# Second feed-forward: block products for three of four up matrices, accumulating weight loads, and the rectified square on ScalarE

## The chip, the core and the metric

One NeuronCore of a Trainium2 chip runs the whole kernel. Its engines are TensorE (PE in the profile, with its weight loads as PEld), VectorE (DVE), ScalarE (ACT), GpSimd (POOL) and SyncE (SP), which here only issues transfers. The metric is the device time of one execution in microseconds, the median of several runs.

## What is computed

The program is two transformer blocks on 512 tokens of width 1024, in float32. Only the second feed-forward, its last stage, is touched:

```
h = rms_norm(x, norm_mlp)                                  # 512 x 1024
x = x + square(relu(h @ w_up)) @ w_down                    # w_up 1024 x 4096, w_down 4096 x 1024
return rms_norm(x, norm_final)
```

where `rms_norm(x, g)` is `x * rsqrt(mean(x * x) + 1e-6) * g`, row by row.

## The kernel before

**Precision.** Every float32 matrix is split into a high part, rounded to the format fp32r (a copy by ScalarE, `..._hi`), and the rest (the difference, by VectorE, `..._lo` or `..._rest`). A product is then three matmuls, high by high, low by high and high by low (`three`, lines 1471 to 1475), so each weight panel costs ScalarE one 128 x 1024 copy and VectorE one 128 x 1024 subtraction before TensorE may use it. The split weights stand in a ring of four slots (`RING`): the copy for a panel waits until the panel four places earlier has been used (`panel_done`).

**Chunks.** The 4096 hidden features are taken in four chunks of 1024 (`CHUNKS2`). A chunk has two phases.

- *Up*: eight panels `Up2(c, u)`. Panel u gives 128 features by 512 tokens: eight groups of three matmuls with 512 columns (`up`, line 2970). VectorE empties the bank with `up_evac` (line 2518): the maximum with 0 times `rrow`, the row of 1/rms of each token spread over all partitions. ScalarE squares (`square`). After every second panel, `combine` forms four sums of quarters of the activations (by tokens and by features), and `combination_hi`, `single_rest` and `sum_rest` split the seven operands into `xch` and `xcl`.
- *Down*: fourteen units `Unit2(c, j)`, which are seven block products in two halves A and B, in the order P1A, Q5A, P1B, Q5B, P6A, P6B, P2A, P2B, P7A, P7B, Q3A, Q3B, R4A, R4B. Seven products of half-size blocks take the place of eight (a scheme of Strassen's kind, with sums of weight blocks by `raw_sum`, line 2548, and sums of activations). Each unit is twelve matmuls with 512 columns. Partial results are copied from bank to bank by ScalarE (`seed`, line 2061, for which P6A waits) and added into the residual `y` by VectorE (`take`, line 2557).

**The first chunk** has more in it. After the last residual sum TensorE forms the column sums of squares, GpSimd raises them to the power -1/2, and `row(5)` spreads the result over the partitions with four transposes inside panel 2. `turn_x` transposes the residual x into token rows after panels 3 to 6 (eight transposes each), which ScalarE copies to `y`.

**Order.** All queues are written out by hand: each engine runs its list in order and waits on semaphores. SyncE loads the panels of `w_up` into four `stage` buffers (512 KB each) and the quarters of `w_down` into `raw` (1 MB each). GpSimd does no transfers.

## Time and profile before

| | |
|---|---|
| median of 3 runs | 1464.92 us (1464.87 to 1464.98) |
| the profiled execution | 1464.81 us |
| its span, first to last instruction | 1463.1 us |
| mean granted TensorE clock | 0.997 |
| TensorE, VectorE, ScalarE busy | 1451.8, 1046.4, 647.5 us |
| first up panel of the second feed-forward to the last matmul | 1124.7 to 1456.2 us of the span |

A row of a group of instructions gives the line, engine and operation, the tiles, the shapes, the count, the busy time in us and the mean duration in ns, and behind the second bar the idle time of the engine just before them with what ended it. A timeline row gives start and duration in us. Matmuls are pipelined: one lasts longer than the distance to the next, and that distance is what it costs in a stream. The same holds to a smaller degree on VectorE and ScalarE.

### The profile page before, as it was taken

To read this page: it belongs to the slowest core of one execution; us is meant where nothing else is said; L and a number is where in the kernel's file an instruction comes from. 1 tells how busy PE (TensorE), PEld (TensorE's weight loads), DVE (VectorE), ACT (ScalarE), POOL (GpSimd) and SP (SyncE) were. 2 spreads that over 40 slices of the span, in tenths; PEclk is the share of its full clock that TensorE was granted. 3 is DMA by queue.
4 is the path that set the end of the run, shared out by engine and by line. 5 is a ranking of instruction groups with operands and counts; after the bars stand their busy time and mean duration, and the time that the engine had idled before them with its cause. 6 is when DMAs were issued, how large, how long until landed. Compare 5 with 4: busy or idle time off the path is not lost.

```text
span 1463.1 us, 20051 instructions
## 1 busy us (share of the span) xinstructions
PE 1451.8 (99%) x7504; PEld 1219.1 (83%) x7504; DVE 1046.4 (72%) x1601; ACT 647.5 (44%) x923; POOL 21.6 (1%) x22
## 2 busy tenths in 40 slices
PE   9999999999999999999999999999999999999998
PEld 7878788888889888988888888888888888888886
DVE  5837764676578577767968887957656686868677
ACT  5214554324434344334634655525444543535354
POOL 0000000000000000000000000000000000000000
PEclk9999999999999999999999999999999999999999
DMA  6623222323520531430233333223215333050401
GB/s 224 247 86 101 79 71 87 92 89 106 210 87 31 186 90 41 135 97 29 86 116 87 119 96 119 73 61 124 72 32 160 142 115 116 36 181 15 173 1 58
DMA packets 38850, 148.93 MB, mean 102 GB/s; under 512 B 4168, under 2 KB 4680, under 8 KB 35572
## 3 DMA queue, kind: packets, MB, share of 16 engines
q1 hardware_dynamic: 34656, 137.90, 29.2%
q10 hardware_dynamic: 4116, 9.96, 2.0%
q8 instruction: 53, 0.87, 0.2%
q14 instruction: 25, 0.20, 0.0%
HBM read 145.72 MB, written 6.06 MB: 104 GB/s over the span
## 4 chain that ended last, share of the span: by engine, by line
PE 96%; DVE 2%; issue 1%; DMA 1%; ACT 0%; SPq 0%; POOLq 0%; ACTq 0%; POOL 0%; DVEq 0%
PE ps L1473 30%; PE ps L1474 30%; PE ps L1475 30%; PE ps L1624 1%; PE ps L1637 1%; PE ps L2834 1%; PE ps L1514 0%; DMA tables<-tables_dram 0%; DVE hl L992 0%; DMA wgu<-wgu_dram 0%; PE ps L1507 0%; PE ps L2854 0%; DVE y L2561 0%; PE ps L2994 0%; PE ps L2866 0%
## 5 line engine op out<-in xcount | busy, mean ns | idle before, releaser
L1473 PE MATMUL ps<-hh,wh 128*128 128x512 f32 x1088 | 431.4, 397 | 0.0
L1474 PE MATMUL ps<-hl,wh 128*128 128x512 f32 x1088 | 424.3, 390 | 0.0
L1475 PE MATMUL ps<-hh,wl 128*128 128x512 f32 x1088 | 424.2, 390 | 0.0
L1473 PEld LDWEIGHTS ps<-hh,wh 128*128 128x128 f32 x1088 | 204.6, 188 | 45.6 <-issue 3.9
L687 ACT ACTIVATE wh<-stage 128x1024 fp32r<-128x1024 f32 x130 | 137.1, 1057 | 234.5 <-PE ps L1475 230.1
L1475 PEld LDWEIGHTS ps<-hh,wl 128*128 128x128 f32 x1088 | 204.5, 188 | 43.5
L1474 PEld LDWEIGHTS ps<-hl,wh 128*128 128x128 f32 x1088 | 204.8, 188 | 39.6
L981 DVE TENSOR_TENSOR wl<-stage,wh 128x1024 fp32r<-128x1024 f32 x129 | 157.4, 1222 | 45.5 <-ACT wh L687 45.2
L2036 ACT ACTIVATE wh<-raw 128x1024 fp32r<-128x1024 f32 x56 | 59.4, 1060 | 73.6 <-PE ps L1475 73.5
L1475 PE MATMUL ps<-xch,wl 128*128 128x256 f32 x308 | 87.2, 283 | 0.0
L1474 PE MATMUL ps<-xcl,wh 128*128 128x256 f32 x308 | 87.2, 283 | 0.0
L1473 PE MATMUL ps<-xch,wh 128*128 128x256 f32 x308 | 87.1, 283 | 0.0
L1473 PE MATMUL ps<-wh,xch 128*128 128x512 f32 x224 | 87.1, 389 | 0.0
L1474 PE MATMUL ps<-wl,xch 128*128 128x512 f32 x224 | 87.1, 389 | 0.0
L1475 PE MATMUL ps<-wh,xcl 128*128 128x512 f32 x224 | 87.1, 389 | 0.0
L858 ACT ACTIVATE wh<-stage 128x1024 fp32r<-128x1024 f32 x40 | 42.3, 1060 | 83.0 <-PE ps L1475 82.3
L2515 DVE TENSOR_TENSOR wl<-raw,wh 128x1024 fp32r<-128x1024 f32 x56 | 68.1, 1222 | 14.3 <-ACT wh L2036 13.9
L986 DVE TENSOR_TENSOR tmp<-ps,rrow 128x512 f32<-128x512 f32 x54 | 37.2, 689 | 54.6 <-PE ps L1475 50.8
L866 ACT ACTIVATE wh<-raw 128x1024 fp32r<-128x1024 f32 (+1 forms) x42 | 40.9, 984 | 53.2 <-PE ps L1475 51.2
L1282 DVE TENSOR_TENSOR wl<-stage,wh 128x1024 fp32r<-128x1024 f32 x40 | 49.0, 1225 | 19.0 <-ACT wh L858 19.0
L1474 PEld LDWEIGHTS ps<-xcl,wh 128*128 128x128 f32 x308 | 59.1, 192 | 0.1
L1473 PEld LDWEIGHTS ps<-xch,wh 128*128 128x128 f32 x308 | 59.1, 192 | 0.1
(372 smaller groups left out, 2577.2 us busy)
## 6 DMA issues: line engine op xcount, KB each, us to landing
stage<-stream_dram SPq DMA_DIRECT2D x198, 512.0 KB, 3.7
raw<-down_dram SPq DMA_DIRECT2D x24, 1024.0 KB, 6.7
bias_lines<-bias_line ACTq DMA_DIRECT2D x1, 3840.0 KB
raw<-down_dram SPq DMA_DIRECT2D x4, 768.0 KB, 5.0
bias<-bias_lines ACTq DMA_DIRECT2D x4, 512.0 KB, 5.0
out_dram<-scaled SPq DMA_DIRECT2D x4, 512.0 KB, 3.0
x<-x_dram SPq DMA_DIRECT2D x3, 512.0 KB, 7.5
bias<-bias_lines ACTq DMA_DIRECT2D x4, 256.0 KB, 2.8
```

Source lines behind the costliest of these rows:

```text
L687: A(parts_of(b, p)[0], b.stage[:, p.stage, :], ACT.Copy).then_inc(s.hi_ready, 1)
L858: A(b.wh[:, p.slot, :], b.stage[:, p.stage, :], ACT.Copy).then_inc(s.hi_ready, 1)
L866: A(b.wh[:, p.slot, 0:p.width], b.raw1[:, QUARTER[p.j], p.half, 0:p.width], ACT.Copy).then_inc(s.hi_ready, 1)
L981: V.tensor_tensor(wl, b.stage[:, p.stage, :], f32(wh), ALU.subtract).then_inc(s.lo_ready, 1)
L986: V.tensor_tensor(dst, b.ps[:, slot, :], b.rrow[:], ALU.mult).then_inc(s.evac, 1)
L1282: V.tensor_tensor(b.wl[:, p.slot, :], b.stage[:, p.stage, :], f32(b.wh[:, p.slot, :]), ALU.subtract).then_inc(s.lo_ready, 1)
L1473: MM(out, wh, xh, start=start, stop=False, skip_group_check=True)
L1474: MM(out, wh, xl, start=False, stop=False, skip_group_check=True)
L1475: return MM(out, wl, xh, start=False, stop=stop, skip_group_check=True)
L1624: ins = MM(b.ps[:, 4 + 2 * (qb % 2) + c, 0:width], q[part, tok], k[part, 0:width], start=n == 0, stop=n == 2, skip_group_check=True)
L2036: A(b.wh[:, p.slot, :], b.raw[:, QUARTER[p.j], p.half, :], ACT.Copy).then_inc(s.hi_ready, 1)
L2515: V.tensor_tensor(b.wl[:, p.slot, :], b.raw[:, QUARTER[p.j], p.half, :], f32(b.wh[:, p.slot, :]), ALU.subtract).then_inc(s.lo_ready, 1)
```

## The change

Chunk 0 keeps its form; chunks 1 to 3 get a new up phase, and the scale of the norm is moved.

- **Up phase of chunks 1 to 3.** Instead of eight panels, two groups g = 0, 1 of seven block products each, `Block2(c, g, product)`, in the order P1, Q5, P6, P2, P7, Q3, R4. The factors are blocks of `w_up` or their sums, and quarters of h by tokens and features or their sums (`xsh`, `xsl`). A product is eight groups of three matmuls with 256 columns into one bank. ScalarE copies banks (`block_seed`, `block_copy`), VectorE takes two differences (`block_take`), and the four results are rectified and squared on ScalarE (`rectify_bank`, `rectify_taken`). Then `block_sums` and the splits `block_singles_hi`, `block_sums_hi`, `block_singles_rest`, `block_sums_rest` make the operands of the down phase. Those of group 1 run at the start of the down phase.
- **Sums of h.** In chunk 0 ScalarE scales x by `norm_mlp` in place (`scale_x`, eight operations), VectorE forms four sums of quarters (`x_sums`), and `x_sums_hi` (4 copies of 128 x 1024) and `x_sums_rest` (4 subtractions) split them.
- **Weight sums.** For chunks 1 to 3, up and down, a half needs four sums: two are now made by transfers that add to their target, issued by GpSimd (`add_first`, `add_third`, 512 KB each), two by VectorE (`second_sum`, `fourth_sum`). SyncE loads five plain transfers of 512 KB for each half.
- **Scale.** The up panels are no longer multiplied by `rrow`. ScalarE rectifies straight from the bank, and `take` multiplies by 1/mean (`r2`, `nr2`) for each token, as two operations of 512 columns instead of one of 1024. `row(5)`, its power on GpSimd and the wait of the first evacuation for it are gone. `turn_x` moves to the places after panels 0 to 3. `grow` is loaded in the last chunk.

```diff
+def weight_block(b, p):
+    if p.product in (Q5, P6):
+        return b.raw_sum[:, p.half, :]
+    return b.raw[:, {P1: 0, P7: 1, Q3: 2, P2: 3, R4: 3}[p.product], p.half, :]
...
 # SyncE, chunks 1 to 3 (the loads of the next up weights in the down phase are alike)
+        for h in range(2):
+            sp.wait_ge(s.lo_ready, Block2(c, h, P1).index + 1)
+            block(c, h, True, 0)
+            sp.wait_ge(s.summed.sem, s.summed.at(summed_by(Block2(c, h, R4), R4)))
+            base(c, h, True)
+            for r, product in ((1, P7), (2, Q3), (3, R4)):
+                sp.wait_ge(s.lo_ready, Block2(c, h, product).index + 1)
+                block(c, h, True, r)
...
 # GpSimd
+    def add_first(c, h, unit):
+        lap = 2 * (c - 1) + unit
+        pool.wait_ge(s.base_in[h].sem, s.base_in[h].at(16 * lap + 16))
+        if lap:
+            pool.wait_ge(s.added_in[h], 32 * lap)
+        G.dma_start(b.raw_sum[:, h, :], weights(c, h, unit, 1), accum_op=ALU.add).then_inc(s.added_in[h], 16)
...
 # ScalarE, chunk 0
+        if u in (4, 5):
+            for k in range(4 * (u - 4), 4 * (u - 4) + 4):
+                scale_x(k)
+        if u in (6, 7):
+            x_sums_hi(2 * (u - 6))
+            x_sums_hi(2 * (u - 6) + 1)
...
 # ScalarE, chunks 1 to 3, one group
+            block_seed(at(P1))
+            block_hi(at(P7))
+            if before:
+                block_sums_hi(before, 0)
+            block_copy(at(Q5), BANK_D[g], 0)
+            block_hi(at(Q3))
+            if before:
+                block_sums_hi(before, 1)
+            block_copy(at(P6), BANK_B[g], 1)
+            block_hi(at(R4))
...
 # ScalarE, after group 1
+        last = Block2(c, 1, R4)
+        block_hi(Unit2(c, P6A))
+        block_sums_hi(last, 0)
+        block_hi(Unit2(c, P6B))
+        block_sums_hi(last, 1)
         seed(c)
...
 # VectorE, chunk 0 (loop over the eight panels), and after it
+        if u == 6:
+            x_sums()
+    for n in range(4):
+        x_sums_rest(n)
+    unit_lo(Unit2(0, P6A))
...
 # VectorE, after group 1
+        block_sums(last, 0)
+        block_singles_rest(last)
+        block_lo(Unit2(c, Q5B))
+        block_sums_rest(last, 0)
+        second_sum(Unit2(c, Q5B))
+        block_lo(Unit2(c, P6A))
+        block_sums(last, 1)
+        block_lo(Unit2(c, P6B))
...
 # TensorE, one group
+                block(c, g, P1, opens=True)
+                pe.wait_ge(s.taken.sem, s.taken.at(6 * (c - 1) + 4 + g))
+                block(c, g, Q5, opens=True)
+                pe.wait_ge(s.block_copied.sem, s.block_copied.at(3 * n + 1))
+                block(c, g, P6)
+                block(c, g, P2)
+                pe.wait_ge(s.block_copied.sem, s.block_copied.at(3 * n + 3))
+                block(c, g, P7)
+                block(c, g, Q3)
+                pe.wait_ge(s.block_taken.sem, s.block_taken.at(2 * n + 1))
+                block(c, g, R4)
```

How the queues read at three places follows, the tiles by their names and the semaphores that a row waits for in brackets.

**ScalarE, chunk 0, panels 6 and 7, before.** `wh` is the high part of a weight block, `mix<-tmp` the square, `xch<-mix` the splits, `y<-ps` the copy of turned x:

```order
L2036 ACTIVATE wh<-raw 128x1024 [waits panel_done,x_raw_in0]
L2045 ACTIVATE mix<-tmp 128x512 [waits act2_ready,evac]
L2059 ACTIVATE y<-ps 128x1024 [waits line_done_x_turned]
L2036 ACTIVATE wh<-raw 128x1024 [waits panel_done,v_normed_summed,x_raw_in0]
L2045 ACTIVATE mix<-tmp 128x512 [waits evac]
L2052 ACTIVATE xch<-mix 128x768 [waits acted2]
L2054 ACTIVATE xch<-mix 128x1024 [waits va_gelu_combined]
```

The same place now. `tmp<-ps` is the new rectification, `xsh<-x` the new copies of the sums of h:

```order
L2135 ACTIVATE wh<-raw 128x1024 [waits panel_done,x_raw_in0]
L2157 ACTIVATE tmp<-ps 128x512 [waits acted2,panel_done]
L2162 ACTIVATE mix<-tmp 128x512 [waits act2_ready,evac]
L2185 ACTIVATE xsh<-x 128x1024 [waits lo_ready,acted]
L2185 ACTIVATE xsh<-x 128x1024
L2135 ACTIVATE wh<-raw 128x1024 [waits panel_done,v_normed_summed,x_raw_in0]
L2157 ACTIVATE tmp<-ps 128x512 [waits acted2,panel_done]
L2162 ACTIVATE mix<-tmp 128x512 [waits evac]
L2168 ACTIVATE xch<-mix 128x768 [waits acted2]
L2170 ACTIVATE xch<-mix 128x1024 [waits va_gelu_combined]
L2185 ACTIVATE xsh<-x 128x1024 x2
```

Between the square of panel 6 and the weight copy of panel 7 there are now two copies that wait for `x_sums` of VectorE (semaphore `acted`).

**ScalarE, end of the up phase of chunk 1, before** (`ps<-ps` is `seed`):

```order
L2045 ACTIVATE mix<-tmp 128x512 [waits evac]
L2052 ACTIVATE xch<-mix 128x768 [waits acted2]
L2054 ACTIVATE xch<-mix 128x1024 [waits va_gelu_combined]
L2036 ACTIVATE wh<-raw 128x1024 [waits panel_done,v_normed_summed,x_raw_in0] x2
L2068 ACTIVATE ps<-ps 128x1024 [waits ln_pow_taken,panel_done]
L2036 ACTIVATE wh<-raw 128x1024 [waits panel_done,x_raw_in3] x2
```

The same place now (`block` holds the four results of a group, `spare1` and `spare2` the sums of them):

```order
L2236 ACTIVATE xch_155<-block_167 128x2x768 [waits acted2]
L2150 ACTIVATE wh_53<-raw_sum_166 128x1024 [waits panel_done,added_in1]
L2150 ACTIVATE wh_53<-raw_sum_166 128x1024 [waits panel_done,v_normed_summed]
L2243 ACTIVATE xch_155<-spare1_168 128x2x2x256 [waits va_gelu_combined]
L2150 ACTIVATE wh_53<-raw_sum_166 128x1024 [waits panel_done,v_normed_summed]
L2243 ACTIVATE xch_155<-spare2_169 128x2x2x256 [waits va_gelu_combined]
L2195 ACTIVATE ps<-ps 128x1024 [waits conved,ln_pow_taken,panel_done]
L2150 ACTIVATE wh_53<-raw_161 128x1024 [waits panel_done,x_raw_in3]
```

Two weight copies and two splits stand now ahead of `seed`; the second split waits for a sum of VectorE (`combined`).

**VectorE, the same place, now** (before, the two weight differences of P6A and P6B followed the last `sum_rest` at once):

```order
L2802 TENSOR_TENSOR spare1_168<-block_167 128x2x256 [waits acted2]
L2803 TENSOR_TENSOR spare1_168<-spare1_168,block_167 128x2x256 [waits steps]
L2793 TENSOR_TENSOR xcl_156<-block_167,xch_155 128x2x768 [waits act2_hi]
L2736 TENSOR_TENSOR wl_54<-raw_sum_166,wh_53 128x1024 [waits hi_ready]
L2817 TENSOR_TENSOR xcl_156<-spare1_168,xch_155 128x2x2x256 [waits act2_hi,va_gelu_combined]
L2743 TENSOR_TENSOR raw_sum_166<-raw_sum_166,raw_161 128x1024 [waits load2]
L2736 TENSOR_TENSOR wl_54<-raw_sum_166,wh_53 128x1024 [waits hi_ready]
L2807 TENSOR_TENSOR spare2_169<-block_167 128x2x256 [waits va_gelu_combined]
L2809 TENSOR_TENSOR spare2_169<-block_167,spare1_168 128x2x256 [waits steps]
L2736 TENSOR_TENSOR wl_54<-raw_sum_166,wh_53 128x1024 [waits hi_ready]
```

The sum for which that second split waits (`spare2`, row 9) has eight operations ahead of it since the last square.

## Rows read from the trace of the kernel before

**Rows 1.** The page: busy time of TensorE, and the chain that ended last.

```profile
PE 1451.8 (99%) x7504; PEld 1219.1 (83%) x7504; DVE 1046.4 (72%) x1601; ACT 647.5 (44%) x923; POOL 21.6 (1%) x22
...
PE 96%; DVE 2%; issue 1%; DMA 1%; ACT 0%; SPq 0%; POOLq 0%; ACTq 0%; POOL 0%; DVEq 0%
```

**Rows 2.** What TensorE waited for, the whole span (total, times, longest, in us).

```profile
PE ps L1530 <- DVE rrow L1007: 1.6, 1, 1.6
```

**Rows 3.** Timeline of the down phase: start, duration in us; matmuls with 512 columns.

```profile
1260.21 0.19 PEld L1474 LDWEIGHTS ps<-wl,xch 128*128 128x128 f32 x1
1260.43 0.39 PE L1474 MATMUL ps<-wl,xch 128*128 128x512 f32 x1
...
1262.70 0.39 PE L1475 MATMUL ps<-wh,xcl 128*128 128x512 f32 x1
```

**Rows 4.** Timeline of TensorE, first feed-forward: products with 256 columns.

```profile
450.03 0.28 PE L1473 MATMUL ps<-xch,wh 128*128 128x256 f32 x1
...
454.71 0.28 PE L1473 MATMUL ps<-xch,wh 128*128 128x256 f32 x1
```

**Rows 5.** Timeline of TensorE around `row(5)` in chunk 0.

```profile
1137.11 0.60 PE L1514 MATMUL ps<-consts,small 128*128 128x128 f32 x4
1137.46 0.48 PE L1473 MATMUL ps<-hh,wh 128*128 128x512 f32 x1
```

**Rows 6.** Timeline of VectorE, end of the up phase of chunk 0.

```profile
1173.36 0.69 DVE L2525 SCALAR_TENSOR_TENSOR tmp<-ps,rrow 128x512 f32<-128x512 f32 x1 [2.81 <-PE ps L1475]
...
1176.35 0.42 DVE L2534 TENSOR_TENSOR mix<-mix 128x256 f32<-128x256 f32 x1
1176.80 0.42 DVE L2535 TENSOR_TENSOR mix<-mix 128x256 f32<-128x256 f32 x1
...
1180.29 2.35 DVE L2515 TENSOR_TENSOR wl<-raw,wh 128x1024 fp32r<-128x1024 f32 x2
```

**Rows 7.** Timeline of ScalarE, the same stretch.

```profile
1177.26 1.06 ACT L2054 ACTIVATE xch<-mix 128x1024 fp32r<-128x1024 f32 x1 [1.36 <-DVE mix L2535]
1178.23 2.15 ACT L2036 ACTIVATE wh<-raw 128x1024 fp32r<-128x1024 f32 x2
1181.52 1.01 ACT L2068 ACTIVATE ps<-ps 128x1024 f32<-128x1024 f32 x1 [1.15 <-PE ps L1475]
```

**Rows 8.** Groups of VectorE from 1120 us on: busy us, mean ns of one.

```profile
L2515 DVE TENSOR_TENSOR wl<-raw,wh 128x1024 fp32r<-128x1024 f32 x56 | 68.1, 1222 | 14.3 <-ACT wh L2036 13.9
...
L2525 DVE SCALAR_TENSOR_TENSOR tmp<-ps,rrow 128x512 f32<-128x512 f32 x32 | 21.9, 688 | 47.7 <-PE ps L1475 41.8 <-ACT rrow L703 5.8
...
L2539 DVE TENSOR_TENSOR xcl<-mix,xch 128x768 fp32r<-128x768 f32 x16 | 15.2, 951 | 0.0
...
L998 DVE TENSOR_TENSOR sumsq<-sumsq,tmp 128x512 f32<-128x512 f32 x2 | 1.4, 685 | 0.0
```

**Rows 9.** Groups of ScalarE from 1120 us on.

```profile
L2036 ACT ACTIVATE wh<-raw 128x1024 fp32r<-128x1024 f32 x56 | 59.4, 1060 | 73.6 <-PE ps L1475 73.5
...
L2045 ACT ACTIVATE mix<-tmp 128x512 f32<-128x512 f32 x32 | 19.9, 621 | 6.7 <-DVE tmp L2525 6.7
...
L2052 ACT ACTIVATE xch<-mix 128x768 fp32r<-128x768 f32 x16 | 13.6, 848 | 0.5
```

**Rows 10.** Busy time and granted clock (PEclk) of TensorE in stretches of the opening.

```profile
5.06:8.47 3.41, 1.86 (x5) 1.00 1.03 385
8.47:11.88 3.41, 3.41 (x8) 0.50 0.73 292
```

**Rows 11.** Timeline of TensorE in the opening.

```profile
7.68 1.13 PE L1536 MATMUL ps<-onehot,tables 32*12 32x512 f32 x2 [1.55 <-DMA tables<-tables_dram]
...
10.61 0.63 PE L1475 MATMUL ps<-hh,wl 128*128 128x512 f32 x1
11.04 0.63 PE L1473 MATMUL ps<-hh,wh 128*128 128x512 f32 x1
```

**Rows 12.** Transfers from 1150 to 1300 us: count, KB each, us to landing.

```profile
stage<-stream_dram SPq DMA_DIRECT2D x13, 512.0 KB, 3.6
```

More of the change, by code:

```diff
@@ new lines, in quarter, with weights, base, block @@
+    def quarter(r):
+        sp.dma_start(b.raw[:, r, :, :], dram["down2"][0, r]).then_inc(s.raw_in[r].sem, 16)
+    def weights(c, h, unit, r):
+        return dram["down2"][c, r, :, h, :] if unit else dram["up2"][c - 1, h, r]
+    def base(c, h, unit):
+        sp.dma_start(b.raw_sum[:, h, :], weights(c, h, unit, 0)).then_inc(s.base_in[h].sem, 16)
+    def block(c, h, unit, r):
+        sp.dma_start(b.raw[:, r, h, :], weights(c, h, unit, r)).then_inc(s.block_in[h][r].sem, 16)
+    for u in range(RING, KT):
+        up_row(u)
@@ L2068, in seed, with block_seed @@
         A(b.ps[:, 2:4, :], b.ps[:, 0:2, :], ACT.Copy).then_inc(s.seeded.sem, 1)
[L2070 to L2084 removed]
+    def block_seed(p):
+        act.wait_ge(s.panel_done, p.index + 1)
+        act.wait_ge(s.taken.sem, s.taken.at(6 * (p.c - 1) + 4 + p.half))
+        A(b.ps[:, BANK_A[p.half], :], b.ps[:, BANK_B[p.half], :], ACT.Copy).then_inc(s.block_copied.sem, 1)
@@ new lines, in block_sums_hi @@
+    def block_sums_hi(p, first):
+        act.wait_ge(s.combined.sem, s.combined.at(PAIRS2 + 2 * p.number + 1 + first))
+        sums = x_quarters((b.spare1, b.spare2)[first][:])[:, :, 0, 0, :].rearrange("p (b n) c -> p n b c", n=2)
+        A(b.xch[:, 2 * p.half:2 * p.half + 2, 3 + first:7:2, :], sums, ACT.Copy).then_inc(s.act2_hi, 1)
+    for u in range(KT):
+        if u < RING:
+            up_hi(Up2(u + RING))
+        else:
+            unit_hi(Unit2(0, u - RING))
+        square(u)
+        if u % 2:
+            combination_hi(u // 2)
+        if u < TT:
+            copy_x(u)
+        if u in (4, 5):
[4 more added lines that the diff above has]
+            x_sums_hi(2 * (u - 6) + 1)
@@ new lines, in block2_vector @@
+    up_lo(Up2(RING))
+    dve.wait_ge(s.mean_ready, 5)
+    st.link(V.reciprocal(b.r2, b.mean))
+    st.link(V.tensor_scalar(b.nr2, b.r2, -1.0, None, ALU.mult))
+    for u in range(KT):
+        if u >= RING:
+            unit_lo(Unit2(0, u - RING))
+        elif u:
+            up_lo(Up2(u + RING))
+        if u % 2:
+            combine(u // 2)
+            single_rest(u // 2)
+        if u == RING:
+            raw_sum(0, 1, 0, 1)
+        elif u == RING + 1:
+            raw_sum(0, 2, 0, 2)
+        elif u == RING + 2:
+            raw_sum(0, 1, 1, 3)
+        elif u == RING + 3:
+            raw_sum(0, 2, 1, 4)
+        if u % 2:
+            sum_rest(u // 2)
+        if u == 6:
+            x_sums()
@@ new lines, in block2_vector @@
+    for n in range(4):
+        x_sums_rest(n)
+    unit_lo(Unit2(0, P6A))
+    unit_lo(Unit2(0, P6B))
+    unit_lo(Unit2(0, P2A))
+    raw_sum(1, 2, 0, 5)
+    unit_lo(Unit2(0, P2B))
+    raw_sum(1, 2, 1, 6)
+    unit_lo(Unit2(0, P7A))
+    raw_sum(3, 0, 0, 7)
+    dve.wait_ge(s.x_copied.sem, s.x_copied.at(TT))
+    take(0, 1, P6B, early, right, 0, b.nr2)
+    unit_lo(Unit2(0, P7B))
+    raw_sum(3, 0, 1, 8)
+    take(0, 2, Q5B, late, right, 4, b.r2)
+    unit_lo(Unit2(0, Q3A))
+    unit_lo(Unit2(0, Q3B))
@@ L2654, in block2_vector @@
     last_take(0)
[L2655 removed]
+    row_scale(2, 5, 3)
     row_mean(0)
```

540 lines of the change are left out of this document (368 added, 172 removed).

## The prediction

> **What bounds the kernel now.** I read the page first: TensorE is busy for 1451.8 of 1463.1 us and makes up 96% of the chain that ended last [rows 1]. Then its waits: the longest in the whole span is 1.6 us, and none falls in the second feed-forward [rows 2]. So a matmul less is time saved, and every wait that is added on TensorE is time lost. I then looked at how far apart matmuls start, since their durations overlap: with 512 columns 0.227 us (ten distances from 1260.43 to 1262.70) [rows 3], with 256 columns 0.120 us (39 distances from 450.03 to 454.71) [rows 4]. A half-width matmul costs 53% of a full one, not 50%. Last, VectorE and ScalarE, whose work must now fit a shorter phase: the durations of their forms and how they follow each other [rows 6 to 9].
>
> **Part 1, the matmuls.** An up phase had 8 x 8 x 3 = 192 matmuls of 512 columns: 192 x 0.2267 = 43.5 us. It gets 14 x 8 x 3 = 336 of 256 columns: 336 x 0.120 = 40.3 us. Saved: 3.2 us for a chunk, 9.6 us for three. Without `row(5)` the four transposes go, which held the stream for 0.35 us, 0.4 with the slower first distance behind them [rows 5]. `turn_x` and the down phases keep their cost. Sum of this part: -10.0 us.
>
> The Trainium skill, "TensorE: Matmul & The Clock Gate", section "Back-to-back issue gap", gives N/2.4 + 2.5 ns: 109 ns for 256 columns, 216 for 512. By it a chunk would save 41.5 - 36.7 = 4.8 us. The trace has both shapes and does not agree; its 0.120 and 0.227 are used.
>
> **Rules for the hand-over.** Operations of one queue follow faster than they last: two of 1024 elements take 2.35 us on VectorE (1.13 apart) [rows 6] and 2.15 on ScalarE; there I use 0.97 apart, from 1177.26 to 1178.23 [rows 7]. One that needs its predecessor's result starts when that ends (1176.35 to 1176.80) [rows 6]. From the end of a VectorE or ScalarE operation to the matmul that it releases I take 0.27 us: 0.05, and 0.22 from weight load to matmul [rows 3]. A consumer sees a panel as done 0.2 us after TensorE has started the next. Durations: VectorE 1.22 (1024), 0.95 (768), 0.69 (512) [rows 8]; ScalarE 1.06, 0.85, 0.62 [rows 9]. The operations of 1536 elements are in no row; from the slopes I take 1.75 and 1.48 us.
>
> **Part 2, the sums of h in chunk 0.** Panel 6 is seen done at about 1167.3. ScalarE is then still scaling x (four operations, to 1169.2), copies the weights of unit P1B (1170.2), rectifies and squares (1171.3), and then waits for `x_sums`. VectorE has the weight difference (1171.4) and one weight sum (1172.6) ahead of it; `x_sums` is four dependent operations of 1024 elements, 5.0 us: to 1177.5. ScalarE then does two copies (1179.5), the weights of Q5B (1180.5), and only now rectifies and squares panel 7 (1181.7), which TensorE finished at 1172.7. Before, VectorE evacuated panel 7 at 1173.36 [rows 6]. Then come `combine` (1183.3) and `single_rest` (1184.1). TensorE begins the down phase at 1172.7, does P1A and Q5A, and half of P1B to 1179.5; the other half needs this split: 1184.1 + 0.27 = 1184.4. **Wait 1: 4.9 us.** P1B and Q5B end at 1188.5. P6A needs its `unit_lo`, which stands behind `single_rest`, a weight sum, `sum_rest` (1186.4) and the four `x_sums_rest` (4 x 1.13, to 1190.9): it ends at 1192.0, TensorE goes on at 1192.3. **Wait 2: 3.8 us.** Behind it VectorE keeps ahead: P7A's difference ends at 1198.8 and its `take` at 1201.2, wanted at 1203. Together +8.7 us. Nothing hides them, since the queues wait for this work alone.
>
> **Part 3, group 1 of each new up phase.** Zero is the moment at which R4 of group 0 is seen done. Group 0's last square ends at 1.25 (0.60 + 0.62 in sequence), `block_sums(0)` at 2.7. VectorE then has: the difference for P2 (its copy ends at 3.7, behind `block_singles_hi`) 5.0, `block_singles_rest` 6.7, `block_sums_rest(0)` 7.8, the difference for P7 8.9, `block_sums(1)` 10.2. ScalarE waits with `block_sums_hi(1)` for that: 11.3, then `block_copy` of P6: 11.85. P7 needs this copy; TensorE would reach P7 at 4 x 2.88 - 0.2 = 11.3, and gets it at 12.1. **Wait 3: 0.8 us, three times.** In group 0 the two splits are absent and the copy ends at 9.2: no wait.
>
> **Part 4, `seed` in the down phase of chunks 1 to 3.** Zero is the end of group 1 as seen by the others. VectorE: `block_sums(0)` 2.7, `block_singles_rest` 4.6 (P1B wants it at 5.2), difference Q5B 5.7, `block_sums_rest(0)` 6.9, `second_sum` 8.1, difference P6A 9.2, `block_sums(1)` 10.5. ScalarE: `block_sums_hi(1)` 11.6, `seed` (1.01 us [rows 7]) 12.55. P6A waits for `seed`, and TensorE reaches it at 4 x 2.72 - 0.2 = 10.7, gets it at 12.8. **Wait 4: 2.2 us, three times.** Before, `seed` ran as soon as P1B was done, at 1181.52 of chunk 0 [rows 7]. Together parts 3 and 4 cost 3.0 us a chunk, +9.0 us: nearly the whole gain of 9.6. In the rest of the down phase the differences are ready 2 us or more ahead.
>
> **Part 5, edits costed at nothing.** `take` as two operations of 512 (2 x 0.69 instead of 1.22 us) and the rectification on ScalarE stand where these engines are ahead; at the end of the kernel the last step is one operation of 512 as before. `row(5)`'s chain on GpSimd had no one behind it but the first evacuations. The queue of SyncE moves five transfers of 512 KB for a half and GpSimd's two more, where it was 2 MB for a half; a plain one lands in 3.6 us [rows 12]. The tightest use of an accumulating one is Q5B of the down phase: `fourth_sum` of group 1 ends at 11.4, the base lands at 15.1, and the copy for Q5B wants the sum at 23.6. So it may take 8.5 us, over twice a plain one. No row shows such a transfer: its cost to the end lies between 0 and what rival 2 gives, and I take 0, as the plain one is nearest.
>
> The Trainium skill, "DMA: Bandwidth & Descriptors", section "Anatomy of one DMA — SWDGE (gpsimd) path", fits 2.0 us + bytes / 436e3 for transfers issued by GpSimd, an estimate of 3.2 us here. By it the cost is 0 as well; whether it holds for an accumulating transfer no row shows.
>
> **Part 6, the clock.** In the opening, TensorE waited 1.55 us up to 7.68, and from 8.47 to 11.88 its granted clock was 0.50, which is 1.2 GHz instead of 2.4 [rows 10, 11]. Matmuls of 512 columns started 0.43 us apart there [rows 11] against 0.227: such a stretch of 3.4 us costs 3.4 x (1 - 0.227/0.43) = 1.6 us. After wait 1 a stretch like this would be hidden, as wait 2 is set by VectorE alone. After wait 2 it would not: +1.6 us, which I take. For the three waits of 2.2 us I take none, up to 3 x 1.6 = 4.8.
>
> **Sum**, against the profiled execution of 1464.81 us (span 1463.1, 1.7 around it; the median 1464.92 is 0.1 above): -10.0 + 8.7 + 9.0 + 1.6 = +9.3, so 1474.1 us.
>
> **Rivals.** (1) *The gain stays.* One mechanism: VectorE does the sums of strided quarters (`x_sums`, `block_sums`) in about half the time of the contiguous rows. Then wait 1 shrinks to 2.4, wait 3 vanishes and wait 4 is 0.8; with wait 2 at 3.8 and no clock stretch: -10.0 + 6.2 + 2.4 = -1.4, 1463.4; if `x_sums_rest`, too, is hidden behind a shorter wait, 1459.6. It decides at 10 us of waits in all. For it: no row has an operation of 4 x 256. Against it: 256, 512, 768 and 1024 elements lie on one line. (2) *Late accumulating transfers.* At 12 us instead of under 8.5, the copy for Q5B comes 3.5 us late and everything behind it on ScalarE, `seed` too: 3 x 3.5 = +10.5, 1484.6. (3) *The clock falls after every `seed`*: +4.8, 1478.9. For it speaks that 1.55 us were enough in the opening; against it, that TensorE ran at full rate right before. (4) *Waits about half as long*, since ScalarE or VectorE hand over sooner than I chain them: -10.0 + 9 = -1, about 1464. (5) The change does what it says but its sums make nothing shorter on TensorE, 256-column matmuls at 0.13 us: 3 x 336 x 0.01 = +10, 1484; rows 4 speak against it, the shape being the same.
>
> **Chances.** Forecast with none or one clock stretch (1471 to 1476): 0.46. Rival 3 or parts of it (1476 to 1481): 0.20. Rivals 2 and 5: 0.08. Rival 4 (1462 to 1468): 0.16. Rival 1: 0.10. A measurement of this kernel tells about 0.2%, 2.9 us, from no change. So slower 0.74, within 0.16, faster 0.10. The range from 1466 to 1481 leaves out rivals 1, 2, 5 and the lower part of 4.
>
> **What would show it.** Right: TensorE waits of 4 to 5 us on VectorE's `xcl` and 3 to 4 us on `wl` near 1180 and 1189 of the span; three of about 2 us on `seed` and three of about 1 us on `diag<-ps`; an up phase of 40.3 us plus 0.8; ScalarE idle for 6 us ahead of `xsh<-x`. Wrong: no wait of TensorE over 1 us in the second feed-forward, strided operations at half the time, or TensorE waiting for a copy that itself waits on GpSimd's queue.

## The result, and the profile after

The changed kernel takes 1477.12 us (median of six runs, 1473.67 to 1478.33), the kernel before 1464.71 (six runs, 1463.06 to 1464.98): a ratio of 1.0084, 95% interval [1.0073, 1.0095]. It is slower by 12.4 us where +9.3 were forecast; the time lies in the range, 3.0 us above the forecast. The profiled execution is the shortest of the six, 1473.67 us with a span of 1471.9. In it the second feed-forward began at 1122.66 us, in the profile of before at 1124.60. That difference of 1.9 us arose ahead of all that was changed, 1.6 of it in the opening, where the profile of before has the wait and the half-clock stretch of [rows 10, 11] and that of after has neither. So the change itself cost 10.7 us between these two profiles. A second profile of the changed kernel, shown with the experiments, began at 1124.64 and cost 11.3. Medians here and below leave out two executions that were slow as a whole: one of experiment 6, 1597.52 us at a mean granted clock of 0.849, and one of the kernel before beside it, 4864.95 us.

From the page after, where [rows 1] stand for before: TensorE is busy 3.9 us less, and still the span is 8.8 us longer.

```profile
span 1471.9 us, 21055 instructions
...
PE 1447.9 (98%) x7932; PEld 1233.0 (84%) x7932; DVE 1065.2 (72%) x1602; ACT 698.1 (47%) x996; POOL 41.3 (3%) x45
...
PE 88%; DVE 6%; DMA 2%; ACT 2%; issue 2%; ACTq 0%; POOLq 0%; POOL 0%; SPq 0%; DVEq 0%
```

The stages of the second feed-forward, each from its first matmul to that of the next, in us. "Reordered" is the kernel of experiment 3.

| stage | before | after | after - before | reordered |
|---|---|---|---|---|
| chunk 0 up | 48.56 | 47.98 | -0.58 | 47.96 |
| chunk 0 down | 38.08 | 47.00 | +8.92 | 38.08 |
| chunk 1 up | 43.52 | 40.83 | -2.69 | 40.32 |
| chunk 1 down | 38.08 | 42.91 | +4.83 | 38.56 |
| chunk 2 up | 43.52 | 40.82 | -2.70 | 40.32 |
| chunk 2 down | 38.08 | 41.57 | +3.49 | 39.16 |
| chunk 3 up | 43.52 | 40.83 | -2.69 | 40.31 |
| chunk 3 down, to its last matmul | 37.86 | 39.78 | +1.92 | 38.42 |
| from there to the end | 7.28 | 7.52 | +0.24 | 7.54 |

The differences sum to +10.7. The up phases gave what they should, the down phases took more than all of it. TensorE in the down phase of chunk 0 and at P6A of chunks 1, 2 and 3, from the timeline (start and duration in us, idle time ahead and its releaser); no such wait was in [rows 2]:

```profile
1182.29 0.80 PE L1574 MATMUL ps<-wh,xch 128*128 128x512 f32 x1 [4.68 <-DVE xcl L2831]
1182.88 0.63 PE L1575 MATMUL ps<-wl,xch 128*128 128x512 f32 x1
...
1190.33 0.47 PE L1574 MATMUL ps<-wh,xch 128*128 128x512 f32 x1 [1.30 <-DVE wl L2730]
...
1272.46 0.61 PE L1574 MATMUL ps<-wh,xch 128*128 128x512 f32 x1 [2.51 <-ACT ps L2195]
...
1356.43 0.50 PE L1574 MATMUL ps<-wh,xch 128*128 128x512 f32 x1 [2.54 <-ACT ps L2195]
...
1437.27 0.50 PE L1574 MATMUL ps<-wh,xch 128*128 128x512 f32 x1 [1.60 <-ACT ps L2195]
```

What stands behind the first two waits is on ScalarE and VectorE. ScalarE first, the same place as [rows 7]: it stands idle for 6.20 us until the last step of `x_sums` is done, and rectifies panel 7 (L2157) at 1178.54, although TensorE had gone on from panel 7 at 1170.64.

```profile
1175.68 2.01 ACT L2185 ACTIVATE xsh<-x 128x1024 fp32r<-128x1024 f32 x2 [6.20 <-DVE x L2761]
...
1178.54 0.57 ACT L2157 ACTIVATE tmp<-ps 128x512 f32<-128x512 f32 x1
```

VectorE in the same stretch, beside [rows 6]: the four steps of `x_sums` from 1170.65 to 1175.65, the split that the second half of P1B waits for (L2831) only at 1181.28, and the four `x_sums_rest` (L2769) ahead of the weight difference of P6A (the first of the three from 1188.96 on).

```profile
1170.65 1.22 DVE L2756 TENSOR_TENSOR x<-x 128x1024 f32<-128x1024 f32 x1
...
1174.42 1.23 DVE L2761 TENSOR_TENSOR x<-x 128x1024 f32<-128x1024 f32 x1
...
1181.28 0.95 DVE L2831 TENSOR_TENSOR xcl<-mix,xch 128x768 fp32r<-128x768 f32 x1
...
1184.42 4.62 DVE L2769 TENSOR_TENSOR xsl<-x,xsh 128x1024 fp32r<-128x1024 f32 x4
1188.96 3.49 DVE L2730 TENSOR_TENSOR wl<-raw,wh 128x1024 fp32r<-128x1024 f32 x3
```

The steps of `x_sums` work on strided quarters and take 1.22 and 1.23 us, as contiguous rows of 1024 elements do [rows 8]. That removes rival 1. The middle two steps, left out here, lie between them.

Last, ScalarE behind group 1: of chunk 1 (the first three lines) and of chunk 3. In chunk 1 the copy for Q5B (L2150) waits 1.21 us for the accumulating transfer. In chunk 3 nothing is late.

```profile
1262.52 2.01 ACT L2150 ACTIVATE wh<-raw_sum 128x1024 fp32r<-128x1024 f32 x2 [1.21 <-DMA raw_sum<-down_dram]
1264.43 1.04 ACT L2243 ACTIVATE xch<-spare 128x1024 fp32r<-128x1024 f32 x1
...
1271.40 1.01 ACT L2195 ACTIVATE ps<-ps 128x1024 f32<-128x1024 f32 x1
...
1429.24 1.04 ACT L2243 ACTIVATE xch<-spare 128x1024 fp32r<-128x1024 f32 x1
1432.78 1.06 ACT L2150 ACTIVATE wh<-raw_sum 128x1024 fp32r<-128x1024 f32 x1 [2.50 <-DVE raw_sum L2743]
1435.24 1.06 ACT L2243 ACTIVATE xch<-spare 128x1024 fp32r<-128x1024 f32 x1 [1.40 <-DVE spare L2809]
1436.21 1.01 ACT L2195 ACTIVATE ps<-ps 128x1024 f32<-128x1024 f32 x1
```

From `block_sums_hi(0)` (the first L2243) to P6A it is 8.03 us in chunk 1 (1264.43 to 1272.46) and 8.03 in chunk 3 (1429.24 to 1437.27). The chain in between is fixed; what differs is when it starts: 5.96 us after the down phase begins in chunk 1, 4.64 in chunk 3.

### The profile page after: what moved, and what is told of

It is laid out like the page before. It is cut to its first block, busy times and chain, and to the rows that moved or that the text cites. A ratio compares the mean times of both kernels' runs of the same rounds, so it can differ in the third digit from the quotient of the medians.

```text
span 1471.9 us, 21055 instructions
## 1 busy us (share of the span) xinstructions
PE 1447.9 (98%) x7932; PEld 1233.0 (84%) x7932; DVE 1065.2 (72%) x1602; ACT 698.1 (47%) x996; POOL 41.3 (3%) x45
## 4 chain that ended last, share of the span: by engine, by line
PE 88%; DVE 6%; DMA 2%; ACT 2%; issue 2%; ACTq 0%; POOLq 0%; POOL 0%; SPq 0%; DVEq 0%
PE ps L1574 28%; PE ps L1576 27%; PE ps L1575 27%; DMA raw_sum<-down_dram 2%; PE ps L1725 1%; PE ps L1738 1%; PE ps L3188 1%; DVE wl L2736 1%; DVE xcl L2817 0%; PE ps L1615 0%; DVE xcl L2793 0%; DMA stage<-stream_dram 0%; DVE hl L1069 0%; DVE y L2851 0%; ACT xch L2236 0%
## 5 line engine op out<-in xcount | busy, mean ns | idle before, releaser
L1574 PE MATMUL ps<-hh,wh 128*128 128x512 f32 (+1 forms) x1040 | 396.7, 381 | 0.2 <-DVE wl L1058 0.2
L1576 PE MATMUL ps<-hh,wl 128*128 128x512 f32 (+1 forms) x1040 | 390.0, 375 | 0.0
L1575 PE MATMUL ps<-hl,wh 128*128 128x512 f32 (+1 forms) x1040 | 389.9, 375 | 0.0
L1574 PEld LDWEIGHTS ps<-hh,wh 128*128 128x128 f32 x1040 | 196.0, 188 | 38.9 <-issue 4.2
L1576 PEld LDWEIGHTS ps<-hh,wl 128*128 128x128 f32 x1040 | 195.8, 188 | 35.7
L1575 PEld LDWEIGHTS ps<-hl,wh 128*128 128x128 f32 x1040 | 196.1, 189 | 32.4
L2736 DVE TENSOR_TENSOR wl<-raw,wh 128x1024 fp32r<-128x1024 f32 x60 | 72.8, 1220 | 27.9 <-ACT wh L2150 27.8
L2150 ACT ACTIVATE wh<-raw 128x1024 fp32r<-128x1024 f32 x60 | 62.6, 1054 | 41.9 <-PE ps L1576 41.5
L1574 PEld LDWEIGHTS ps<-wh,xch 128*128 128x128 f32 x224 | 43.1, 192 | 24.8 <-ACT ps L2195 7.9
```

The costliest lines, as they stand in the source:

```text
L1574: MM(out, wh, xh, start=start, stop=False, skip_group_check=True)
L1575: MM(out, wh, xl, start=False, stop=False, skip_group_check=True)
L1576: return MM(out, wl, xh, start=False, stop=stop, skip_group_check=True)
L2150: A(b.wh[:, p.slot, :], weight_block(b, p), ACT.Copy).then_inc(s.hi_ready, 1)
L2736: V.tensor_tensor(b.wl[:, p.slot, :], weight_block(b, p), f32(b.wh[:, p.slot, :]), ALU.subtract).then_inc(s.lo_ready, 1)
```

## Experiments

The theory: TensorE's part of the change is worth 10 us, as computed, and all that ate it is order. In chunk 0 the sums of x stand ahead of panel 7 and of P6A; in the other chunks `seed` stands last behind group 1. Two more suspects are the late accumulating transfer and the clock behind the waits. Each run changes one of these. All times are medians, beside 1464.6 to 1464.9 us of the kernel before on the same chip. For the changed kernel I use 1477.4, the middle of its two medians (1477.12, and 1477.77 below). A median holds the half-clock stretches of all its runs, wherever they lie, and a profile those of one run; so I also give what a run's profile shows from the first matmul of the second feed-forward to the end of the span. That is 338.5 us before, and 349.3 and 349.7 in the two profiles of the changed kernel.

### 1. `seed` earlier

```diff
         block_hi(Unit2(c, P6A))
         block_sums_hi(last, 0)
+        seed(c)
         block_hi(Unit2(c, P6B))
         block_sums_hi(last, 1)
-        seed(c)
```

> Only the order on ScalarE behind group 1 of chunks 1 to 3 changes: `seed` comes right behind block_sums_hi(0), ahead of the copy for P6B and of block_sums_hi(1). Theory (what is lost there is the place of `seed` in ScalarE's queue): `seed` waits only for P1B, ends about 9.3 us after group 1, TensorE wants it at 10.7, so the three waits of 2.5, 2.5 and 1.6 us on P6A are gone and with them the half-clock stretches behind them (one in the profiled run, 1.7 us; up to three in others). Against the kernel after: -6.7 for the waits, -1.7 to -5.1 for the clock, so about 1467 us, and runs that lie closer together. Rival A (the transfer for Q5B that comes 1.2 us late is what really holds the queue): about half the wait stays, -3.4, 1472 or so. Rival B (the clock falls for another reason than the waits): 6.7 less, but half-clock stretches in chunks 1 to 3 remain.

Measured: 1467.32 us (11 runs, 1465.88 to 1468.76), ratio to before 1.0015 [1.0006, 1.0024], 10.1 us less than the changed kernel. What TensorE waited for, over its whole span (total, times, longest): no `seed` among them.

```profile
PE ps L1574 <- DVE xcl L2831: 4.7, 1, 4.7
...
PE ps L1574 <- DVE wl L2730: 0.9, 1, 0.9
```

The down phases of chunks 1 and 2 take 38.81 and 39.14 us instead of 42.91 and 41.57. The copy for Q5B still waited for its transfer (1.28 us in chunk 1), and P6A did not notice: with `seed` out of that chain the lateness is hidden. The half-clock stretch of chunk 1 is gone, that of chunk 0 is there. From the stage's first matmul to the end the profile has 340.9 us, 8.4 to 8.8 less than the changed kernel's, which is the 6.7 of the waits and one stretch; the further 1.3 us or more of the medians no profile shows. The theory holds; rivals A and B fall.

### 2. The sums of x spread out

```diff
-            x_sums()
-    for n in range(4):
-        x_sums_rest(n)
+            x_sums(0)
+    x_sums(1)
     unit_lo(Unit2(0, P6A))
     unit_lo(Unit2(0, P6B))
+    x_sums(2)
...
     unit_lo(Unit2(0, Q3A))
+    x_sums(3)
...
     unit_lo(Unit2(0, R4A))
+    x_sums_rest(0)
```

The other three splits follow behind R4B's difference and behind P1's and Q5's of chunk 1, `x_sums_hi` on ScalarE likewise, and TensorE waits for them ahead of Q5 of chunk 1.

> Only the sums of x change their place: the four steps of x_sums are spread over VectorE's queue of chunk 0 (behind panel 6, ahead of the difference P6A, behind P6B, behind Q3A), and x_sums_hi and x_sums_rest stand among the work for R4A, R4B, P1 and Q5 of chunk 1, whose first user is Q5 of chunk 1. Theory (ScalarE held by x_sums, and four x_sums_rest ahead of P6A's difference, are the whole loss of chunk 0): waits of 4.7 and 1.3 us gone, the half-clock stretch of 6.8 us gone (worth 3.2 us), so -9.2 against the kernel after's profiled run (1473.7): about 1465; against its median up to 3 us more. Rival A (the same VectorE work only moves the wait to a later take or to chunk 1): a new TensorE wait of some us in P7A, Q3A or at Q5 of chunk 1, and a gain under 5 us. Rival B (TensorE's clock falls anyway, for another reason): -6.0 only, and a half-clock stretch remains near 1180 us.

Measured: 1469.16 us (6 runs, 1468.19 to 1470.28), ratio to before 1.0032 [1.002, 1.0044], 8.2 us less than the changed kernel. The down phase of chunk 0 takes 38.08 us (1172.77 to 1210.85), as before the change, and the up phase of chunk 1 has only the known wait for `diag`. The waits that are left:

```profile
PE ps L1574 <- ACT ps L2195: 6.8, 3, 2.5
...
PE ps L1574 <- DVE xcl L2822: 1.1, 2, 0.8
PE ps L1574 <- ACT diag L2208: 0.8, 3, 0.3
```

So the same eight VectorE operations (four steps of `x_sums`, four splits), with the four copies of ScalarE between them, cost 8.9 us in the one place and nothing in the other. No wait moved to a later unit of chunk 0 or to Q5 of chunk 1, and no half-clock stretch is left near 1180: both rivals fall. The profile as a whole is only 6.8 us shorter in this stage than the changed kernel's first (342.5 us), where 9.2 were expected: two of the three `seed` waits brought a half-clock stretch, where that profile had one, and in chunk 2 there is a wait of 0.84 us on `xcl`.

### 3. Both, and the copy of P6 and `fourth_sum` earlier

```diff
+            block_copy(at(P6), BANK_B[g], 1)
             if before:
                 block_sums_hi(before, 1)
-            block_copy(at(P6), BANK_B[g], 1)
...
+                fourth_sum(at(R4))
                 block_sums(before, 1)
-                fourth_sum(at(R4))
```

> Both changes of order (seed earlier; sums of x spread) and, in group 1 of the up phases, the copy of P6 ahead of block_sums_hi(1) on ScalarE and fourth_sum ahead of block_sums(1) on VectorE. Theory (the matmul part is worth 10.0 us, and everything that ate it is order in the queues of VectorE and ScalarE, plus the clock that falls behind waits): no TensorE wait over 1 us in the second feed-forward, no half-clock stretch there, up phases of 40.3 us: before minus 10.0, 1454.7 us, up to 1456. Rival (the up panels' gain itself is smaller than the spacing of matmuls says, or transfers that come late set new waits): 1460 or more.

Measured: 1456.03 us (5 runs, 1455.4 to 1456.88), ratio to before 0.9941 [0.9928, 0.9955]: faster than both kernels, 8.8 us less than before. That is the upper end of what I expected, and the rival (1460 or more) falls. Of the waits that are left the longest is shown, which lies ahead of the stage, and the longest in the second feed-forward, the last line, 0.35 us in chunk 2:

```profile
PE ps L1631 <- DVE rrow L1084: 1.6, 1, 1.6
...
PE ps L1574 <- DVE xcl L2822: 0.3, 1, 0.3
```

The up phases take 40.32, 40.32 and 40.31 us where 336 x 0.120 = 40.3 was computed, and 43.52 before. The table gives -10.2 us for the matmuls, +2.1 for the down phases of chunks 1 to 3, which are 0.5 to 1.1 us longer than before, and +0.3 at the end: -7.8 between the profiles, where the medians differ by 8.8. In each of these phases the matmuls at two places, 8 to 9 and 22 to 23 us into the phase, start 0.31 to 0.42 us apart instead of 0.227, in chunk 2 also 5.6 us into it, and there the wait of 0.35 us stands. The place at 8 to 9 us can be read from the trace. The copy for Q5B still waits for its accumulating transfer (0.56, 0.82 and 0.64 us in the three chunks), the split of the first sum stands behind it on ScalarE, and VectorE waits for that split. ScalarE, VectorE and TensorE in chunk 2:

```profile
1334.15 2.01 ACT L2150 ACTIVATE wh<-raw_sum 128x1024 fp32r<-128x1024 f32 x2 [0.82 <-DMA raw_sum<-down_dram]
...
1337.20 1.23 DVE L2822 TENSOR_TENSOR xcl<-spare,xch 128x1024 fp32r<-128x1024 f32 x1 [0.74 <-ACT xch L2243]
...
1338.58 0.47 PE L1574 MATMUL ps<-wh,xch 128*128 128x512 f32 x1 [0.35 <-DVE xcl L2822]
```

Which hand-over sets the place at 22 to 23 us I did not test.

### 4. Only the copy of P6 and `fourth_sum` earlier

The diff is that of experiment 3, alone.

> Only two pairs change places in group 1 of the up phases: the copy of P6 ahead of block_sums_hi(1) on ScalarE, and fourth_sum ahead of block_sums(1) on VectorE. Theory: the wait on the copy of P6 (0.26 us, three times) goes, and Q5B's base transfer starts about 1.5 us earlier, so that its accumulating transfer is there before ScalarE wants it; the waits of TensorE on `seed` fall by the lateness of that transfer, about 1.2 us in chunk 1 and less in the others. Together -2 to -3.5 us. Rival (the late transfer costs nothing, the order seed behind block_sums_hi(1) sets it all): waits on `seed` stay at 2.5, 2.5, 1.6 and only 0.8 us is gained; it can't be told from nothing in the time, so the waits in the trace decide.

Measured: 1473.8 us (5 runs, 1471.01 to 1476.19), ratio to before 1.0062 [1.0048, 1.0077]. The wait on `diag` is gone and the up phases take 40.31 us. The time is 3.6 us less than the changed kernel's, but the reason I gave for it is wrong. The copy for Q5B waits less for its transfer, 0.35 us in chunk 1 instead of 1.21, and P6A still waited as long: 2.51, 2.51 and 2.54 us, in chunk 3 even 0.94 more than before this edit. ScalarE behind group 1 of chunk 1, where the down phase begins at 1259.95:

```profile
1260.63 0.58 ACT L2219 ACTIVATE block<-ps 128x512 f32<-128x512 f32 x1
...
1263.62 2.02 ACT L2150 ACTIVATE wh<-raw_sum 128x1024 fp32r<-128x1024 f32 x2 [0.35 <-DMA raw_sum<-down_dram]
1265.54 1.04 ACT L2243 ACTIVATE xch<-spare 128x1024 fp32r<-128x1024 f32 x1
...
1426.69 2.01 ACT L2150 ACTIVATE wh<-raw_sum 128x1024 fp32r<-128x1024 f32 x2 [0.36 <-DMA raw_sum<-down_dram]
```

Two things changed. First, the last rectification (L2219) starts 0.68 us into the phase, in the changed kernel 0.20 (1258.67 against 1258.47). In group 1, `block_sums(1)` now stands 1.2 us later on VectorE, ScalarE waits for it with `block_sums_hi(1)`, and all behind that on ScalarE is later. Second, the transfer gained little: its base is issued 0.8 us earlier, but it lands 3.6 us into the phase of chunk 1 where it was 4.0. In chunk 3 it even comes later than before: 3.6 us into the phase, so that the copy waits for it until 1426.69 (the last line above; the phase begins at 1423.02), where it had landed at 2.5, ahead of ScalarE. From issue to landing it took 6.6 us there in the changed kernel and takes 8.9 us here. SyncE's last plain transfer of the half is now issued 0.1 us behind it and runs beside it; in the changed kernel that one had been issued 1.6 us ahead of it and landed 2.6 us before it. That this is why it took longer is not shown. The 8.02 us from the L2243 to P6A (1265.54 to 1273.56) are as before, so P6A follows the landing: 0.38 us earlier in chunk 1, and in chunk 3 0.93 later (13.60 us into the phase instead of 12.67), some 0.6 by the later ScalarE and 0.36 by the transfer. Between the two profiles, each from the first matmul of its second feed-forward to the end, the difference is 2.6 us, of which the half-clock stretch that this profile lacks in chunk 1 is 1.6. How much of the 3.6 us between medians is this, too, single profiles do not tell.

### 5. The changed kernel once more

> The changed kernel itself, unedited, on the same chip as the three runs beside it: about 1475 to 1477 us, with runs that lie some 4 us apart because the number of half-clock stretches differs from run to run.

Measured: 1477.77 us (5 runs, 1475.93 to 1479.22), ratio to before 1.009 [1.0077, 1.0104]. The median is 0.8 us above what I expected and the runs lie 3.3 us apart. In its profile (span 1474.4) the waits are nearly those of the first (in chunk 2 one of 0.83 us on `xcl` where it was 0.38), with half-clock stretches from 1184.86 and from 1275.23 on, behind the waits of 4.68 and 2.51 us.

### 6. Filler matmuls in the waits of chunk 0 and of `seed`

```diff
+    def keep_busy(n):
+        for _ in range(n):
+            MM(b.ps[:, 6, :], b.xch[:, 0, 0, 0:P], b.xch[:, 0, 0:2, :].rearrange("p n c -> p (n c)"), start=True, stop=True,
+               skip_group_check=True)
...
         for m in (2 * p.half, 2 * p.half + 1):
+            if c == 0 and j == P1B and m == 3:
+                keep_busy(18)
...
+        if c:
+            keep_busy(9)
         pe.wait_ge(s.seeded.sem, s.seeded.at(c + 1))
```

> The kernel after with filler matmuls (operands that lie ready, a bank nobody reads) where TensorE would wait: 18 ahead of the second half of P1B in chunk 0 (18 x 0.227 = 4.1 of its 4.7 us) and 9 ahead of each wait on `seed` (2.0 us of 2.5; of the last one's 1.6 they may cost 0.4). The waits themselves stay. Theory (the clock falls because TensorE stands idle in these waits; behind wait 1 that is hidden, since P6A's difference comes from VectorE at the same moment whatever TensorE does): the half-clock stretch near 1182 us is gone, P6A starts as late as before, 19.7 us after the down phase begins, and its wait grows from 1.3 to about 4 us, behind which a new half-clock stretch of 3.4 us can come (+1.7 us); in chunks 1 to 3 no stretch is left (-1.7 us for each that the kernel after has). Together -1 to -4 us against the median of the kernel after. Rival A (wait 1's half clock was not hidden): P6A starts 3 us earlier, -5 us or more. Rival B (the clock has another cause): the stretches stay, no gain, +0.4.

Measured: 1475.99 us (5 runs, 1474.0 to 1477.01), ratio to before 1.0076 [1.0063, 1.0089], 1.8 us less than the run beside it. TensorE in chunk 0: the down phase began at 1172.95, so P6A starts 19.70 us into it, where it was 19.69 in the unedited kernel beside it (1172.62 to 1192.31).

```profile
1184.61 0.50 PE L1574 MATMUL ps<-wh,xch 128*128 128x512 f32 x1 [0.61 <-DVE xcl L2831]
1192.65 0.47 PE L1574 MATMUL ps<-wh,xch 128*128 128x512 f32 x1 [3.67 <-DVE wl L2730]
...
1194.16 0.63 PE L1574 MATMUL ps<-wh,xch 128*128 128x512 f32 x1
1194.59 0.63 PE L1575 MATMUL ps<-wl,xch 128*128 128x512 f32 x1
```

This is the kernel that the prediction's part 2 had in mind: no half clock behind wait 1, a wait 2 of 3.67 us (3.8 forecast), and then the half-clock stretch, which makes the down phase 48.64 us instead of 46.99: +1.65, where +1.6 was computed. The granted clock (the sixth value behind the length of the stretch, ahead of DMA share and GB/s) between wait 1 and P6A is 1.00 here, 2.4 GHz, and was 0.50 in the changed kernel's first profile, second fence:

```profile
1184.50:1190.00 5.50, 4.37 (x18) 3.30 (x18) 5.50 (x6) 5.50 (x7) 1.94 (x2) 1.00 0.76 186
```
```profile
1180.50:1187.30 6.80, 5.01 (x12) 3.95 (x13) 6.77 (x9) 6.05 (x8) 1.94 (x2) 0.50 0.73 190
```

In chunks 1 to 3 no stretch is left. Rival A (wait 1's half clock was not hidden) and rival B (another cause) fall.

### 7. Fillers ahead of P6A in chunk 0 too

```diff
-        if c:
-            keep_busy(9)
+        keep_busy(9 if c else 17)
```

> As the run with fillers beside it, and 17 more fillers (3.9 us) ahead of P6A in chunk 0, so that no wait of over 0.7 us is left without matmuls in the second feed-forward. Theory (idle waits bring the half-clock stretches, and these are the spread between runs): no half-clock stretch there, time = the kernel after without any stretch, about 1472 us, and all runs within 1 us of each other. Rival (another cause): stretches and the spread of 4 us stay.

Measured: 1473.29 us (6 runs, 1472.11 to 1474.71), ratio to before 1.0062 [1.0049, 1.0074], 4.5 us less than the unedited kernel beside it. No matmul of the second feed-forward runs at half clock. The down phase of chunk 0 takes 47.02 us, again as long as with the stretch behind wait 1. From the stage's first matmul to the end the profile has 347.6 us, 1.7 and 2.1 less than the two of the changed kernel; the rest of the 4.5 us lies in stretches that these profiles do not show.

The time is 1.3 us over what I expected, and the spread of 2.6 us is not the 1 us I expected. The mean granted clock of each run says why. The three of 1472.11 to 1472.84 us had 0.999, the three of 1473.73 to 1474.71 had 0.998. The kernel before in the same batch, without any wait in this stage, had 0.999 in its runs of 1462.92 to 1463.39 us, and 0.998 or 0.997 in those of 1464.46 to 1466.68. So half-clock stretches elsewhere are left, and with them the spread. The profiles show one such place. At 730 us, in a stage that no edit touches, TensorE waits 0.77 or 0.78 us and then runs sixteen matmuls of one column; in seven of the ten profiles a half-clock stretch follows at 731.6 to 733.2, and this profile, which begins the second feed-forward at 1122.82 where its neighbours began at 1124.39 to 1124.96, has none. The wait, and TensorE's clock (the second value behind the length of the stretch) right behind it, in the profile of experiment 5:

```profile
730.23 1.05 PE L3038 MATMUL ps<-consts,sum 128*128 128x1 f32 x8 [0.78 <-DVE sum L1477]
...
732.50:735.50 3.00, 3.00 (x9) 0.50 0.91 302
```

### 8. Plain transfers from GpSimd

```diff
-        G.dma_start(b.raw_sum[:, h, :], weights(c, h, unit, 1), accum_op=ALU.add).then_inc(s.added_in[h], 16)
+        G.dma_start(b.raw_sum[:, h, :], weights(c, h, unit, 1)).then_inc(s.added_in[h], 16)
...
-        G.dma_start(b.raw[:, 1, h, :], weights(c, h, unit, 2), accum_op=ALU.add).then_inc(s.added_in[h], 16)
+        G.dma_start(b.raw[:, 1, h, :], weights(c, h, unit, 2)).then_inc(s.added_in[h], 16)
```

> The transfers issued by GpSimd are plain ones instead of accumulating ones; so the weight sums are left out (raw_sum holds one summand), while every operation and every byte stays. Theory A (the accumulation is what costs: 8.3 us where SyncE's plain transfer of the same 512 KB took 3.9 to 4.8): they land in about 4 to 5 us, the copy for Q5B is not late in chunks 1 and 2 (it was by 1.2 and 1.5 us), `seed` comes about 1.3 us earlier there, span 2.5 us shorter plus or minus a clock stretch. Theory B (GpSimd's queue, or the traffic beside it, is what costs): they still land in about 8 us and nothing moves.

The sums of weight blocks that these transfers form are left out here; every operation and every byte stays. Measured, one run: 1471.52 us, span 1469.8. Transfers (count, KB each, median us to landing) of the changed kernel first, then of this one:

```profile
raw_sum<-up_dram SPq DMA_DIRECT2D x6, 512.0 KB, 3.9
raw_sum<-up_dram POOLq DMA_DIRECT2D x6, 512.0 KB, 8.3
raw<-up_dram POOLq DMA_DIRECT2D x6, 512.0 KB, 8.5
raw_sum<-down_dram SPq DMA_DIRECT2D x6, 512.0 KB, 4.8
raw_sum<-down_dram POOLq DMA_DIRECT2D x6, 512.0 KB, 8.3
raw<-down_dram POOLq DMA_DIRECT2D x6, 512.0 KB, 5.5
```
```profile
raw_sum<-up_dram POOLq DMA_DIRECT2D x6, 512.0 KB, 6.4
raw<-up_dram POOLq DMA_DIRECT2D x6, 512.0 KB, 6.4
raw_sum<-down_dram SPq DMA_DIRECT2D x6, 512.0 KB, 4.7
raw_sum<-down_dram POOLq DMA_DIRECT2D x6, 512.0 KB, 6.7
raw<-down_dram POOLq DMA_DIRECT2D x6, 512.0 KB, 3.9
```

Neither theory has the landing right: it is halfway. Accumulating costs 1.6 to 2.1 us of a transfer, and what is left above SyncE's transfer of the same tile (2.5 us up, 2.0 down) goes with GpSimd's queue or with the moment. The effect on the path is theory A's: P6A starts 12.67 us into the down phase of chunk 1 and 13.27 into that of chunk 2, in the unedited kernel beside it 13.96 and 14.69. So accumulating costs 1.3 and 1.4 us there, and nothing in chunk 3 (12.67 and 12.68). In chunk 2 even the plain transfer is late, and P6A comes 0.60 us behind its place in chunk 3:

```profile
1344.34 2.01 ACT L2150 ACTIVATE wh<-raw_sum 128x1024 fp32r<-128x1024 f32 x2 [0.49 <-DMA raw_sum<-down_dram]
```

From the stage's first matmul to the end this profile has 345.4 us, 4.3 less than the one beside it: these 2.7, and 1.6 for a half-clock stretch that it lacks in chunk 1.

## Why the prediction came out as it did

**What bounds the kernel.** Right. Matmuls less were time saved (experiment 3) and every wait came out in the time.

**Part 1, -10.0.** Right: 3.2 us for an up phase (40.32 against 43.52) and 0.6 for chunk 0's where 0.4 was computed, -10.2 in all. Here row and rule of the Trainium skill ("TensorE: Matmul & The Clock Gate", "Back-to-back issue gap") were weighed: the rule, which that section gives for a single matmul and not for a stream, would have saved 4.8 us for a chunk; these did not come, the 3.2 from the distances in [rows 3, 4] did. Rival 5 is out with it.

**Part 2, +8.7, and part 6, +1.6.** Wait 1 was forecast at 4.9 us and P6A at 19.6 us into the down phase; they came at 4.68 and 19.69. Both reasons hold: chaining ScalarE's and VectorE's queues by hand with the durations of rows gave the place to 0.1 us. What failed is the step in part 6: of wait 1's half-clock stretch it said rightly that it is hidden, but not that by stretching P1B and Q5B it shortens wait 2 from 3.8 us to 1.3. Behind 1.3 us no stretch came. So chunk 0 cost 8.9 and not 10.3; experiment 6 restores the forecast case, with +1.65 behind 3.67 us.

**Part 3, 0.8 us three times.** 0.26 us of waiting and 0.25 more in the spacing around it: 0.5 a chunk by the up phases, 40.83 against 40.32. The mechanism was right (experiments 3 and 4 remove it), its size 0.3 too large. Some 0.2 of that is the hand-over, forecast at 0.27 us from the end of an operation to the matmul that it releases: it measured 0.05 us behind ScalarE (`seed` ends at 1272.41, P6A starts at 1272.46) and 0.15 behind a difference of VectorE (1190.18 to 1190.33).

**Part 4, 2.2 us three times.** In chunk 3, where no transfer is late, P6A starts 12.67 us into the phase. Forecast were 12.8 us behind the moment at which the others see group 1 done, and so 13.0 into the phase: 0.3 too late, by the hand-over again. The wait is 1.6 us and the phase 1.92 us longer than before. In chunks 1 and 2 P6A starts at 13.99 and 14.23.

**Part 5, costed at nothing.** This is the step whose failure cost most. The bound was right: from its base on, an accumulating transfer may take 8.5 us until Q5B's copy hurts, and the real one took 8.2 in chunk 1. But the bound started from a base that lands 3.6 us after its issue, the nearest row, and the real base took 4.7, with 0.3 us more until GpSimd issued the next. Together they came 1.2 us (chunk 1) and 1.5 (chunk 2) late, and P6A 1.3 and 1.6 us later than in chunk 3: +2.9. Experiment 8 shows that most of this goes with the accumulation. Rival 2 had the mechanism, with 12 us instead of 8.3. And the last of the signs of being wrong came in part: TensorE waited for `seed`, and `seed` stood behind a copy that waited for a transfer of GpSimd's. The estimate of 3.2 us from the Trainium skill ("DMA: Bandwidth & Descriptors", "Anatomy of one DMA — SWDGE (gpsimd) path") does not hold here: even the plain transfers that GpSimd issued took 3.9 to 6.7 us.

**The clock behind `seed`.** Rival 3 came in part: one stretch (1.6 us) in both profiles of the changed kernel, not three and not none. The median, 1477.1, lies in the band from 1476 to 1481 that was kept for it with a chance of 0.20, and not in the forecast's own.

**The sum.** By the stages of the first profile: -10.2 for the matmuls, +8.9 for chunk 0, +1.5 for part 3, and +10.2 for the down phases of chunks 1 to 3, which are 2.9 for the late transfer, 1.6 for the clock, and 5.8 for the rest, against the 6.6 of part 4; with 0.2 at the end +10.7. The forecast of +9.3 has 1.4 us too much in chunk 0, 0.9 in part 3, 0.8 in part 4 and 0.2 in part 1, together 3.3; it lacks 2.9, 1.6 and 0.2, together 4.7. That it came so near is thus in part luck: the paths were right, and errors of both signs nearly cancel. The median lies 1.1 us further up than the second profile's +11.3. Half-clock stretches in the other runs would do that, and the mean granted clock points to them: it was 0.995 in the profiled run of 1473.67 us and 0.993 or 0.994 in the other five, and 3.4 us at half clock take 0.001 from it; where in those runs they lie, nothing shows. Rival 4 (waits half as long) fell: parts 2 to 4 cost 16.2 us where 17.7 were forecast.
